# Memory attention of a two-block forward pass: a second transposed buffer, own banks for the scores, and a reordered head loop

## The reference

```
def memory_cross_attention(h, m, w_q, w_kv, w_o):
    b, s, _ = h.shape
    ml = m.shape[1]
    q = (h @ w_q).reshape(b, s, MEM_HEADS, MEM_HEAD_DIM)
    kv = (m @ w_kv).reshape(b, ml, 2, MEM_HEADS, MEM_HEAD_DIM)
    k, v = kv[:, :, 0], kv[:, :, 1]
    sc = jnp.einsum("bqhd,bkhd->bhqk", q, k).astype(jnp.float32) * (MEM_HEAD_DIM ** -0.5)
    p = jax.nn.softmax(sc, axis=-1).astype(v.dtype)
    o = jnp.einsum("bhqk,bkhd->bqhd", p, v).reshape(b, s, MEM_HEADS * MEM_HEAD_DIM)
    return o @ w_o
...
        x = x + (g_conv * y_conv + g_mla * y_mla) @ w_mix_out[l]
        x = x + memory_cross_attention(rmsnorm(x, norm_mem_g[l]), rmsnorm(mem, norm_memkv_g[l]),
                                       w_mem_q[l], w_mem_kv[l], w_mem_out[l])
        x = x + expert_choice_moe(rmsnorm(x, norm_moe_g[l]), w_router[l], w_exp_gate[l],
                                  w_exp_up[l], w_exp_down[l])
```

## Time and profile before

| | |
|---|---|
| median of 3 runs | 2032.77 us (2032.26 to 2033.19) |
| the profiled execution, own time | 2037.77 us |
| its span, first to last instruction | 2036.0 us |
| granted TensorE clock, mean | 0.964 |
| PE busy | 1884.0 us (93%) |
| DVE busy | 844.0 us (41%) |
| ACT busy | 554.6 us (27%) |
| DMA, mean rate | 159 GB/s |

### The profile page before, as it was taken

The page is one execution under the profiler, slowest core; times in us unless marked ns, Lnnn a source line. Parts: engine busy times, 40 slices in busy tenths (PEclk is TensorE's granted clock), DMA queues, the critical chain, the costliest instruction groups (busy, mean ns, idle before and its releaser), DMA issues.

```text
span 2036.0 us, 20712 instructions
## 1 busy us (share of the span) xinstructions
PE 1884.0 (93%) x8786; PEld 1332.1 (65%) x8786; DVE 844.0 (41%) x1089; ACT 554.6 (27%) x729; POOL 0.2 (0%) x4
## 2 busy tenths in 40 slices
PE   5999999999999978999998884999989999999997
PEld 4788666688787663443443331897868778787785
DVE  5544345525563451111111116345754654443445
ACT  4222344433343221111100013234323332223231
POOL 0000000000000000000000000000000000000000
PEclk9999999999999988999999997899987999999999
DMA  4323211032343065999999993222210223232221
GB/s 151 105 83 104 76 33 34 24 124 83 104 146 123 22 265 239 421 421 422 421 421 421 421 421 130 82 63 83 83 63 21 83 83 104 82 97 88 86 97 45
DMA packets 148211, 324.51 MB, mean 159 GB/s; under 512 B 8848, under 2 KB 118432, under 8 KB 123552
## 3 DMA queue, kind: packets, MB, share of 16 engines
q1 hardware_dynamic: 148128, 323.30, 42.7%
HBM read 321.18 MB, written 2.10 MB: 159 GB/s over the span
## 4 chain that ended last, share of the span: by engine, by line
PE 80%; DMA 8%; DVE 7%; ACT 3%; issue 2%; SPq 0%; DVEq 0%; ACTq 0%
PE bank L507 18%; PE bank L509 18%; PE bank L508 18%; PE bank L901 11%; DMA ew_b<-in_w_exp_up 3%; DMA ew_d<-in_w_exp_up 3%; PE bank L866 2%; PE bank L690 1%; PE bank L666 1%; DMA raw<-in_w_exp_up 1%; PE bank L924 1%; DMA ew_d<-in_w_exp_down 1%; DVE w_lo L1547 1%; ACT w_hi L1149 1%; PE bank L1040 1%
## 5 line engine op out<-in xcount | busy, mean ns | idle before, releaser
L507 PE MATMUL bank<-H_hi,w_hi 128*128 128x512 f32 (+1 forms) x896 | 351.2, 392 | 28.1 <-DVE H_lo L1547 25.9
L1547 DVE TENSOR_TENSOR w_lo<-raw,w_hi 128x2048 fp32r<-128x2048 f32 x107 | 245.0, 2291 | 281.0 <-ACT w_hi L1149 255.2
L508 PE MATMUL bank<-H_lo,w_hi 128*128 128x512 f32 (+1 forms) x896 | 345.1, 385 | 0.0
L509 PE MATMUL bank<-H_hi,w_lo 128*128 128x512 f32 (+1 forms) x896 | 344.9, 385 | 0.0
L507 PEld LDWEIGHTS bank<-H_hi,w_hi 128*128 128x128 f32 x896 | 171.1, 191 | 82.8 <-issue 34.2
L509 PEld LDWEIGHTS bank<-H_hi,w_lo 128*128 128x128 f32 x896 | 171.3, 191 | 35.9
L508 PEld LDWEIGHTS bank<-H_lo,w_hi 128*128 128x128 f32 x896 | 171.7, 192 | 34.7 <-issue 0.7
L1149 ACT ACTIVATE w_hi<-raw 128x2048 fp32r<-128x2048 f32 x77 | 146.8, 1907 | 115.5 <-PE bank L509 113.7
L507 PE MATMUL bank<-C_hi,w_hi 128*128 128x512 f32 x384 | 154.2, 401 | 6.8 <-DVE X L2117 6.8
L508 PE MATMUL bank<-C_lo,w_hi 128*128 128x512 f32 x384 | 152.4, 397 | 0.0
L509 PE MATMUL bank<-C_hi,w_lo 128*128 128x512 f32 x384 | 152.4, 397 | 0.0
(11 more groups left out here) (354 smaller groups left out, 2556.2 us busy)
## 6 DMA issues: line engine op xcount, KB each, us to landing
raw<-in_w_in SPq DMA_DIRECT2D x38, 1024.0 KB, 5.5
raw<-in_w_ff SPq DMA_DIRECT2D x32, 1024.0 KB, 5.3
ew_b<-in_w_exp_gate SPq DMA_DIRECT2D x16, 1024.0 KB, 26.4
ew_b<-in_w_exp_up SPq DMA_DIRECT2D x16, 1024.0 KB, 26.1
ew_c<-in_w_exp_up SPq DMA_DIRECT2D x16, 1024.0 KB, 26.9
ew_b<-in_w_exp_down SPq DMA_DIRECT2D x16, 1024.0 KB, 26.6
ew_c<-in_w_exp_gate SPq DMA_DIRECT2D x16, 1024.0 KB, 27.8
ew_c<-in_w_exp_down SPq DMA_DIRECT2D x16, 1024.0 KB, 27.6
```

The costliest lines, as they stand in the source:

```text
L507: pe.matmul(o, lhs[0], rhs[0], start=first, stop=False)
L508: pe.matmul(o, lhs[0], rhs[1], start=False, stop=False)
L509: return pe.matmul(o, lhs[1], rhs[0], start=False, stop=last)
L1547: return dve.tensor_tensor(out=dst, in0=src, in1=hi_part.bitcast(F32), op=ALU.subtract)
```

## The change

1. `mpt` gets a second buffer, by h % 2.
2. The scores leave the rotation: head h writes banks 4 and 5 (h even) or 6 and 7 (h odd). From head 2 on they wait for the exponentials of head h-2.
3. The loop over heads is written out in all three queues. PE: S0, S1, T0, S2, V0, T1, S3, V1, T2, T3, V2, V3. ACT and DVE have the same order for their parts.
4. `norm_sums("mem")` on PE comes behind memkv unit 1 instead of 0, and `root`, `norm_start`, `his` and `norm_split` come one turn later.
5. In the memkv turns ACT does `split_hi` ahead of the second tile's copy instead of behind it.

No instruction is added or dropped; the same transfers are made.

```diff
-        mpt = place("mpt", [P, 2, S], F32, R + 56 * K)
+        mpt = place("mpt", [P, 2, 2, S], F32, R + 56 * K)
...
                 dense_tiles(U0["memkv"] + i, "mk", 2 * i, MEM, M, lambda m: (mkv_ready, m + 1),
                             ready=(mem_lo_ready, 0))
-                if i == 0:
+                if i == 1:
                     norm_sums("mem")
...
                 for j in range(2):
-                    o = tile((mexp_done, 4 * h + 2 * j + 2))
+                    if h >= 2:
+                        pe.wait_ge(mexp_done, 4 * (h - 2) + 2 * j + 2)
+                    marks.tile = o = bank[4 + 2 * (h % 2) + j]
...
+            mem_scores(0)
+            mem_scores(1)
+            mem_turn(0)
+            mem_scores(2)
+            mem_values(0)
+            mem_turn(1)
+            mem_scores(3)
+            mem_values(1)
+            mem_turn(2)
+            mem_turn(3)
+            mem_values(2)
+            mem_values(3)
...
+                    if j:
+                        split_hi(U0["memkv"] + i + 2)
                     act.activation(dst, o[:, 0:UC], ACT.Copy).then_inc(mkv_ready, 1)
-                split_hi(U0["memkv"] + i + 2)
-                if i == 0:
+                if i == 1:
                     root("mem")
-                if 1 <= i <= 4:
-                    his("mem", (2 * i - 2, 2 * i - 1))
+                if 2 <= i <= 5:
+                    his("mem", (2 * i - 4, 2 * i - 3))
...
                 split_lo(U0["memkv"] + i + 2)
-                if i == 0:
+                if i == 1:
                     norm_start("mem")
-                if 1 <= i <= 4:
-                    norm_split("mem", "norm_mem_g", (2 * i - 2, 2 * i - 1))
+                if 2 <= i <= 5:
+                    norm_split("mem", "norm_mem_g", (2 * i - 4, 2 * i - 3))
```

More of the change, by code:

```diff
@@ L786, in mem_scores, with mem_turn @@
                     mark(ins, ("msc", h, j))
[L788 to L791, removed]
+            def mem_turn(h):
                 for j in range(2):
@@ L797, in _, with mem_values @@
                     mark(ins, ("mpt", h, j))
+            def mem_values(h):
                 for i in range(2):
@@ L802, in _ @@
                         c = h * MEM + i * P
-                        ins = pe.matmul(o[:, :], mv[:, j, c:c + P], mpt[:, j, :], start=(j == 0), stop=(j == 1))
+                        ins = pe.matmul(o[:, :], mv[:, j, c:c + P], mpt[:, h % 2, j, :], start=(j == 0), stop=(j == 1))
                     mark(ins, ("mpv", h, i))
+            mem_scores(0)
[10 more added lines that the diff above has]
+            mem_values(3)
             pe.wait_ge(router_in, 32)
@@ L1339, in mem_exps, with mem_turned, mem_valued @@
                                    accum_out=sm[:, s:s + 1]).then_inc(mexp_done, 1)
[L1341 to L1344, removed]
+            def mem_turned(h):
                 o = done(act, ("mpt", h, 0))
-                act.activation(mpt[:, 0, :], o[:, :], ACT.Copy).then_inc(mpt_0, 1)
+                act.activation(mpt[:, h % 2, 0, :], o[:, :], ACT.Copy).then_inc(mpt_0, 1)
+            def mem_valued(h):
                 for i in range(2):
@@ L1349, in _ @@
                     act.activation(H_hi[:, 2 * h + i, :], o[:, :], ACT.Copy).then_inc(mo_hi_ready, 1)
+            mem_exps(0)
+            mem_exps(1)
+            mem_turned(0)
+            mem_exps(2)
+            mem_valued(0)
+            mem_turned(1)
+            mem_exps(3)
+            mem_valued(1)
+            mem_turned(2)
+            mem_turned(3)
+            mem_valued(2)
+            mem_valued(3)
             for i in range(2):
@@ L1789, in mem_softmax, with mem_turned, mem_valued @@
                                       ALU.mult).then_inc(mp_ready, 1)
[L1791 to L1794, removed]
+            def mem_turned(h):
                 o = done(dve, ("mpt", h, 1))
-                dve.tensor_copy(mpt[:, 1, :], o[:, :]).then_inc(mpt_1, 1)
+                dve.tensor_copy(mpt[:, h % 2, 1, :], o[:, :]).then_inc(mpt_1, 1)
+            def mem_valued(h):
                 for i in range(2):
@@ L1800, in _ @@
                     rest(H_lo[:, 2 * h + i, :], o[:, :], H_hi[:, 2 * h + i, :]).then_inc(mo_lo_ready, 1)
+            mem_softmax(0)
+            mem_softmax(1)
+            mem_turned(0)
+            mem_softmax(2)
+            mem_valued(0)
+            mem_turned(1)
+            mem_softmax(3)
+            mem_valued(1)
+            mem_turned(2)
+            mem_turned(3)
+            mem_valued(2)
+            mem_valued(3)
             for i in range(4):
```

## The result

| | before | changed |
|---|---|---|
| median of 6 runs | 2033.0 us (2032.3 to 2038.0) | 2018.87 us (2017.5 to 2021.3) |
| ratio, 95% interval | | 0.9921 (0.9911 to 0.9931) |
| the profiled execution, own time | 2037.77 us | 2017.52 us |
| its span | 2036.0 us | 2015.7 us |

The change is faster by 0.79% by the ratio, which is 16.1 us; 15.9 were forecast. The two medians differ by 14.1 us, the means of the same runs by 15.4: four of the six runs of before lie between 2032.3 and 2033.2, and two near 2038. Beside the later experiments the kernel before had medians of 2035.9, 2035.1 and 2036.8 us, and beside the last of them the changed kernel was 16.7 us faster by the medians (e10). So the gain is 14 to 17 us, depending on which runs of before it is taken from.

The account below looks back on a forecast made before the run. PE was taken as the bound, with its waits and lowered clock in memkv and the head loop. Gains of 7.6 and 8.3 us, 15.9 in all, take the median 2032.8 to 2016.9 us; 8-in-10 range 2014.0 to 2022.0.

Parts of the forecast that it names:

- Part A: memkv stretch, edits 4 and 5: PE loses its stop before the sums and memq starts 7.6 us earlier.
- restart behind fp32 work: memkv, end of unit 2: 0.3 us charged to PE on top of the two sums' 1.75 us.
- The ring: memkv: ACT and DVE wait on each other through splits, scaling, his and copies, setting the pace; 6.40 us instead of 6.67.
- Part B: Head loop, edits 1 to 3: PE's waits for copies into mpt go, 32.7 us instead of 41.0, so 8.3 us.
- The meetings: Head loop, T3 and V2: DVE's results come within 0.2 us of when PE wants them; 0.2 us charged.
- the clock's share: Head loop, V0: at granted clock 0.67 it takes 5.20 us instead of 3.51; full clock wins 1.7 us.
- Behind it: Stages after mem_out: expert loads and router work shift with PE, so no loss of the gain is charged.
- Rival 1: Head loop: the second buffer only moves PE's waits, only the clock's 1.7 us is won, time 2023.5 us; chance 7%.
- The case of the Trainium skill's page: Head loop: as in that page's kernel, double-buffering gives nothing, leaving only the memkv gain, 2025.2 us.
- Rival 2: memkv: gain lost to late reciprocal or loads, PE's 6.35 us return as waits, time 2024.5 us; chance 6%.
- rival 3: Expert stage: the whole gain is given back there, time 2032.8 us, no change; chance 3%.
- Rival 4: Head loop: clock falls in T0 and stays at half through the loop, 7.8 us slower, 2040.6 us; chance 2%.

Follow-up runs that it names:

- e10: The changed kernel run and profiled again, nothing altered: median 2020.03 us, ratio to the kernel before 0.9920.
- e3: The changed kernel with split_hi put back behind both copies in the memkv turns: 2021.36 us, ratio to the kernel before 0.9932.
- e9: The kernel before plus three unread fp32 matmuls behind T0, where PE waits: loop 39.28 us; a single run of 2034.91 us against a median of 2036.76.
- e4: The kernel before plus 15 unread matmuls ahead of the sums, where PE waits: 2033.17 us against 2035.91, ratio 0.9983.
- e5: The changed kernel with a single mpt buffer and the order's end made T2, V2, T3, V3: 2019.63 us, ratio to the kernel before 0.9927.
- e6: The changed kernel with the scores back in the rotation over banks 0 to 3: 2021.03 us, ratio to the kernel before 0.9934.
- e2: The kernel before with only edits 1 to 3 (second mpt buffer, own score banks, new head order): 2027.27 us, ratio 0.9953.
- e1: The kernel before with only edits 4 and 5 (later sums, earlier split in memkv): 2028.67 us against 2035.91, ratio 0.9962.

## Why the prediction was right

**What bounds the kernel.** Right: PE's stops and its clock. DVE's and ACT's busy times stayed (844.0 and 843.7 us, 554.6 and 553.9), the time fell.

**Part A, 7.6 us forecast, 7.84 measured.** The steps stand as put, apart from two sizes. PE goes from unit 0 into unit 1 without a stop. Unit 2 starts at 561.38 (forecast 561.65), because I charged the restart behind fp32 work twice: V3 reaches `mem_out`'s first row in 3.11 us before (687.94 to 691.05), 0.40 short of its 3.51, and it is that first row which is longer. So the 1.75 us of the sums held the restart of 0.3 already; measured, it is 1.48 to the first row, which is 0.23 longer than its successors (0.51 against 0.28). The ring is there with the forecast period: 567.50, 573.97, 580.37, 586.76, 593.16, so 6.47 and three times 6.40. memq starts at 597.44 (forecast 597.7). The split edit was sized at 1.0, for four turns, and is worth 1.44 (e3), since it also lies on the path to unit 2. The reciprocal was covered, by 1.85 us (forecast 2).

**Part B, 8.3 us forecast, 8.78 measured.** V0 starts 12.46 us into the loop (forecast 12.5). The loop takes 32.20 us (forecast 32.7): the transposes of a head take 0.87 to 0.88 from start to start, not 0.95, scores 3.45 and values 3.43. The meetings were as near as forecast and cost 0.3 us (0.2 charged): T2 and T3 take 2.07 us from 666.00 to V2, not twice 0.87. The clock stayed at 1.00; its share of 1.7 was measured by e9 (40.98 to 39.28). That e4's V0 paid 2.8 us for the same stop shows that the 1.7 is the price in one execution.

**The sources within part B**, the clock's share apart, were not forecast, and here the experiments add something. Of part B's 8.8 us, 0.9 are the buffer (e5) and 1.7 the clock (e9). The remaining 6.1, by subtraction, are the order and the banks together: without banks of their own for the scores 3.1 us go back (e6). These shares overlap: of the 3.1, too, 1.75 are the clock.

**Behind it.** Right: from `mem_out` to the first expert load every kernel takes 48.95 to 48.97 us. The profile pair's other 3.8 us (2.8 to the down load, 1.0 behind it) go with no edit and are not in the medians; their cause was not found. Who had explained the spans' 20.3 us by the change would have been wrong by a fifth.

**The rivals.** Rival 1 fell with e2: no wait came back that the rows show. The case of the Trainium skill's page "TensorE: Matmul & The Clock Gate", section "HAM oscillation — how this bites in real kernels", in which double-buffering PSUM brought no further gain, does not carry over: the PSUM banks of the scores' own are worth 3.1 us here (e6). The second `mpt` buffer, which lies in SBUF and not in PSUM, is worth 0.94 (e5). Rival 2 fell with e1, rival 3 with the 48.96 us and the time. Rival 4, the clock, had its place right and not its length: with one stop of 1.18 us behind T0 it did fall (e6), and was back before V0, which took 3.43 us. In the changed kernel nothing but T0's own waits was left there, and it did not fall.

**The time.** That the ratio's 16.1 us meet the forecast's 15.9 so closely is partly luck. The two stages won 16.6 in the profiles, 0.7 more than forecast, by small misses that mostly went one way, and the comparisons of times range from 14.1 to 16.7. The base moved as well: the three runs shown of before were all near 2032.8, and later ones went to 2038.4, so that the median of 2018.87 lies 2.0 above 2016.9 although the stages won more than was said. The mechanism is confirmed by the stage lengths, not by the closeness of the total.

## What to carry to other kernels

Where an in-order engine waits for a copy, look for a block of its own work that can stand in the gap and ask what that block needs: here the larger part of the gain is what the new order is left with, 3.1 us of the 8.8 hung on banks of its own for the scores, and 0.94 on the second buffer. Price a stop of PE at its length and at what the clock adds behind it: where it fell, that was 1.4 to 2.8 us for stops of 1.2 to 3.5 us, and it differed between executions. And compare two profiles by stages that end at the same event: of a difference of 20.3 us between two spans, 16.5 lay ahead of the first expert load behind `mem_out`, where the changed kernel's second profile agreed with its first to 0.01 us and the two parts alone gave 7.7 and 8.7, and the rest went with no edit.

## What the runs showed of the hardware

- Behind the same stop (2.58 us) the same V0 took 5.20 us in the kernel before and in e1, and 6.29 in e4, where the granted clock over it was 0.55 instead of 0.67. With all code up to its end unchanged, memkv took 56.58 us in the one execution and 55.33 in the other (e9). So the price of one and the same stop was not fixed; what sets it, no run shows.
- The clock fell behind a stop of 1.18 us in e6, when PE had done eight spaced transposes (2.05 us) before it, and did not fall behind 1.75 us in the kernel before, when it had done eight in 1.04 us. So the length of the idle time alone does not tell whether the clock falls.
- Extra matmuls in a stop made the kernel faster by 0.17% (e4, interval 0.08 to 0.27%).
